# Compression's first product on four column groups of the tensor engine, its partial sums turned and added by one product with a constant

## The reference, cut to what matters

```
nc = (256 - 32) // 16 + 1                       # 15 windows of 32 tokens, 16 apart
def compress(t, pe, w1, w2):                    # t: 256 tokens x 64
    blocks = (t[:, win_idx] + pe).reshape(b, nc, 32 * 64)          # 15 x 2048
    return gelu(blocks @ w1, approximate=False) @ w2               # w1: 2048 x 256, w2: 256 x 64
kc = compress(k_cmp, pe_k, w1_k, w2_k)
vc = compress(v_cmp, pe_v, w1_v, w2_v)
```

## Time and profile before

| | us |
|---|---|
| median of three runs | 2038.98 (2037.13 to 2039.16) |
| the profiled execution | 2038.0 |
| its span | 2036.1 |
| PE busy | 1990.1 (98% of the span) |
| PEld busy | 1821.0 (89%) |
| POOL busy | 1282.7 (63%) |
| DVE busy | 1244.7 (61%) |
| ACT busy | 992.0 (49%) |
| line 659 on PE, 128 matmuls | 29.0 |
| transfers, mean | 166 GB/s |

### The profile page before, as it was taken

How to read it: one execution, slowest core, us unless ns; L and a number is a source line. 1 busy time by engine, 2 the same in 40 slices (tenths; PEclk the granted TensorE clock), 3 DMA queues, 4 the chain that set the end, 5 groups by cost and what they waited for, 6 DMA issues and landing times.

```text
span 2036.1 us, 41550 instructions
## 1 busy us (share of the span) xinstructions
PE 1990.1 (98%) x14222; PEld 1821.0 (89%) x14222; DVE 1244.7 (61%) x2722; ACT 992.0 (49%) x1557; POOL 1282.7 (63%) x622
## 2 busy tenths in 40 slices
PE   9999999999999999999999999999999999999998
PEld 9798998999999888888897889999999998888886
DVE  4463399449999544444454624993599994444444
ACT  5545444654443545544555444446444444455444
POOL 6346689876766555555463466998766665555553
PEclk9999999999999999999999999999999999999999
DMA  6524554554444555556545245545444445555554
GB/s 213 164 92 135 177 175 162 179 169 145 146 141 143 185 195 194 189 194 195 186 142 164 82 148 185 172 160 184 165 146 143 145 142 190 194 193 192 192 196 134
DMA packets 93242, 338.45 MB, mean 166 GB/s; under 512 B 10352, under 2 KB 10736, under 8 KB 93168
## 3 DMA queue, kind: packets, MB, share of 16 engines
q1 hardware_dynamic: 93168, 337.53, 49.8%
HBM read 336.44 MB, written 1.05 MB: 166 GB/s over the span
## 4 chain that ended last, share of the span: by engine, by line
PE 91%; POOL 3%; issue 2%; DVE 2%; ACT 1%; DMA 1%; POOLq 0%; SPq 0%; DVEq 0%; ACTq 0%
PE PS L915 34%; PE PS L852 11%; PE PS L857 11%; PE PS L853 11%; PE PS L551 5%; PE PS L866 4%; POOL WL L454 3%; PE PS L535 2%; PE PS L540 2%; PE PS L536 2%; PE PS L777 2%; PE PS L659 1%; PE PS L517 1%; PE PS L588 1%; PE PS L620 0%
## 5 line engine op out<-in xcount | busy, mean ns | idle before, releaser
L454 POOL TENSOR_TENSOR WL<-ring,WH 128x1024 fp32r<-128x1024 f32 x360 | 908.9, 2531 | 413.6 <-ACT WH L1149 207.9
L1149 ACT CAST WH<-ring 128x1024 fp32r<-128x1024 f32 x512 | 538.0, 1051 | 706.1 <-PE PS L915 327.0
L484 POOL TENSOR_TENSOR HL<-G,HH 128x256 fp32r<-128x256 f32 x256 | 372.6, 1456 | 324.1 <-ACT HH L1251 324.0
L1766 DVE TENSOR_TENSOR WL<-ring,WH 128x1024 fp32r<-128x1024 f32 x248 | 303.8, 1225 | 370.9 <-ACT WH L1149 370.9
L852 PE MATMUL PS<-HH,WH 128*128 128x256 f32 x2048 | 512.2, 288 | 0.0
L853 PE MATMUL PS<-HL,WH 128*128 128x256 f32 x2048 | 501.3, 283 | 0.0
L853 PEld LDWEIGHTS PS<-HL,WH 128*128 128x128 f32 x2048 | 392.2, 192 | 0.0
L852 PEld LDWEIGHTS PS<-HH,WH 128*128 128x128 f32 x2048 | 391.2, 191 | 0.0
L915 PE MATMUL PS<-WH,HH 128*128 128x512 f32 x1024 | 315.5, 389 | 3.0 <-issue 3.0
L915 PE MATMUL PS<-WH,HL 128*128 128x512 f32 x1024 | 315.3, 389 | 0.0
L1715 DVE SCALAR_TENSOR_TENSOR OH<-IOB,slotT,PS 128x384 bf16<-128x384 bf16 x512 | 308.0, 602 | 0.0
(11 more groups left out here) (244 smaller groups left out, 2195.0 us busy)
## 6 DMA issues: line engine op xcount, KB each, us to landing
ring<-stream SPq DMA_DIRECT2D x636, 512.0 KB, 3.3
X<-x_t SPq DMA_DIRECT2D x4, 256.0 KB, 3.5
out_t<-X SPq DMA_DIRECT2D x2, 512.0 KB, 2.7
CN<-consts SPq DMA_DIRECT2D x1, 843.5 KB, 9.4
WF<-last SPq DMA_DIRECT2D x1, 512.0 KB, 9.8
PR<-params SPq DMA_DIRECT2D x2, 239.0 KB, 5.0
CN<-consts SPq DMA_DIRECT2D x1, 64.0 KB, 4.3
```

The source lines that it names most:

```text
L454: nc.gpsimd.tensor_tensor(WL[:, b, :], ring[:, slot, :], WH[:, b, :].bitcast(F32), ALU.subtract).then_inc(done, 1)
L484: nc.gpsimd.tensor_tensor(GL[:, s, :], G[:, tile, :], GH[:, s, :].bitcast(F32), ALU.subtract).then_inc(L.gl_ready, 1)
L1149: nc.scalar.copy(WH[:, b, :], ring[:, slot, :]).then_inc(L.hi_ready, 1)
L1766: V.tensor_tensor(WL[:, s % 2, :], ring[:, (U0 + s) % SLOTS, :], WH[:, s % 2, :].bitcast(F32), ALU.subtract).then_inc(L.vlo_ready, 1)
```

## The change

The four chunks of a piece now go to four groups of 32 columns of the array (`tile_position`), and so to partitions 0 to 14, 32 to 46, 64 to 78 and 96 to 110 of bank 7. Each group adds up its own chunk of the four pieces. Each product now writes 32 partitions, since `BL` is widened from 15 to 32 columns, of which 17 are zero, set by POOL at the layer's start (one more memset, and one more wait on PE for it). The four partial sums have to be added before the gelu. So ACT first copies all 128 partitions of bank 7 to `HID`; behind projection 11 PE multiplies `HID` by a constant 128 x 15 with ones where partition mod 32 equals the window (`sum4`), which turns and adds in one; the gelu moves to the two instructions that fill `HV`.

```diff
@@ shape_constants
+    put("sum4", p % 32 == np.arange(NCMP)[None, :])
@@ POOL, start of a layer
+                    nc.gpsimd.memset(BL[:, :, :, NCMP:32], 0.0).then_inc(padded, 1)
                     nc.gpsimd.memset(HV[:, :, :, :, :], 0.0).then_inc(padded, 1)
@@ PE
                         pe.wait_ge(L.blocks_ready, i + 1)
-                        o = bank[7][0:NCMP, i * 256:(i + 1) * 256]
+                        pe.wait_ge(padded, 2 * layer + 1)
                         for k in range(4):
                             w = piece(2 * W1 + 4 * i + k).rearrange("p (j m) -> p j m", j=CHUNKS // 4)
                             for j in range(CHUNKS // 4):
-                                mm = nc.tensor.matmul(o, BL[:, i, CHUNKS // 4 * k + j, :], w[:, j, :],
-                                                      start=(k == 0 and j == 0), stop=(k == 3 and j == CHUNKS // 4 - 1))
+                                mm = nc.tensor.matmul(bank[7][32 * j:32 * j + 32, i * 256:(i + 1) * 256],
+                                                      BL[:, i, CHUNKS // 4 * k + j, :], w[:, j, :],
+                                                      start=(k == 0), stop=(k == 3), tile_position=(0, 32 * j))
...
                     for i in range(4):
-                        mm = nc.tensor.transpose(bank[7][:, 16 * i:16 * i + NCMP],
-                                                 HID[0:NCMP, i // 2, i % 2 * P:(i % 2 + 1) * P], ident[0:NCMP, 0:NCMP])
+                        mm = nc.tensor.matmul(bank[7][:, 16 * i:16 * i + NCMP],
+                                              HID[:, i // 2, i % 2 * P:(i % 2 + 1) * P], cn("sum4"), start=True, stop=True)
@@ ACT
                     act.wait_ge(L.piece_done, 2 * W1 + 8)
-                    nc.scalar.activation(HID[0:NCMP, :, :], bank[7][0:NCMP, :].rearrange("p (s n) -> p s n", s=2),
-                                         ACT.Gelu).then_inc(L.hid_ready, 1)
+                    nc.scalar.copy(HID[:, :, :], bank[7].rearrange("p (s n) -> p s n", s=2)).then_inc(L.hid_ready, 1)
                     take(11)
...
-                    nc.scalar.copy(HV[:, 0, :, 0, 0:NCMP], hid[:, 0]).then_inc(L.hid_ready, 1)
-                    nc.scalar.copy(HV[:, 1, :, :, 0:NCMP], bc(hid[:, 1], 2, NH)).then_inc(L.hid_ready, 1)
+                    nc.scalar.activation(HV[:, 0, :, 0, 0:NCMP], hid[:, 0], ACT.Gelu).then_inc(L.hid_ready, 1)
+                    nc.scalar.activation(HV[:, 1, :, :, 0:NCMP], bc(hid[:, 1], 2, NH), ACT.Gelu).then_inc(L.hid_ready, 1)
```

More of the change, by code:

```diff
@@ L89 @@
                       ("cr", 128), ("sr", 128), ("c16", 32), ("s16", 32), ("cmpneg", 64), ("any", 2),
-                      ("blkd", 4), ("iota", 129)):
+                      ("blkd", 4), ("sum4", 15), ("iota", 129)):
     CONSTS[_name] = (_at, _at + _width)
@@ L332, in program @@
         K2 = region(2 * SEQ).rearrange("p (s n) -> p s n", s=2)
-        BL = region(2 * CHUNKS * NCMP).rearrange("p (s j c) -> p s j c", s=2, j=CHUNKS)
+        BL = region(2 * CHUNKS * 32).rearrange("p (s j c) -> p s j c", s=2, j=CHUNKS)
         HV = region(2 * 2 * P).rearrange("p (s b h c) -> p s b h c", s=2, b=2, h=NH)
@@ L1078, in _ @@
                     act.wait_ge(L.piece_done, 2 * W1 + 8)
-                    nc.scalar.activation(HID[0:NCMP, :, :], bank[7][0:NCMP, :].rearrange("p (s n) -> p s n", s=2),
-                                         ACT.Gelu).then_inc(L.hid_ready, 1)
+                    nc.scalar.copy(HID[:, :, :], bank[7].rearrange("p (s n) -> p s n", s=2)).then_inc(L.hid_ready, 1)
                     take(11)
-                    act.wait_ge(padded, layer + 1)
+                    act.wait_ge(padded, 2 * layer + 2)
                     act.wait_ge(hid_tr, layer + 1)
                     hid = bank[7][:, 0:64].rearrange("p (s b c) -> p s b c", s=2, b=2)[:, :, :, 0:NCMP]
-                    nc.scalar.copy(HV[:, 0, :, 0, 0:NCMP], hid[:, 0]).then_inc(L.hid_ready, 1)
-                    nc.scalar.copy(HV[:, 1, :, :, 0:NCMP], bc(hid[:, 1], 2, NH)).then_inc(L.hid_ready, 1)
+                    nc.scalar.activation(HV[:, 0, :, 0, 0:NCMP], hid[:, 0], ACT.Gelu).then_inc(L.hid_ready, 1)
+                    nc.scalar.activation(HV[:, 1, :, :, 0:NCMP], bc(hid[:, 1], 2, NH), ACT.Gelu).then_inc(L.hid_ready, 1)
                     probabilities(PT[0])
@@ L1462, in _ @@
                             src = k2[:, 0, :, hi:hi + NCMP]
-                            ins = V.tensor_tensor(BL[:, s, 8 * hi:8 * hi + 8, :], src,
+                            ins = V.tensor_tensor(BL[:, s, 8 * hi:8 * hi + 8, 0:NCMP], src,
                                                   bc(pr(pe_name, 8 * hi, 8 * hi + 8), 2, NCMP), ALU.add)
```

## The result

The changed kernel takes 2041.68 us in the median of 20 runs (2037.91 to 2045.06), the kernel before, measured beside it, 2037.93 (2036.90 to 2040.28, 20 runs). The ratio is 1.0019, 95% interval [1.0013, 1.0026]: slower by 3.9 us by the ratio, where 3.6 us less were forecast. The time lies inside the range, within 0.1 us of the rivals "the clock" and "no overlap" (2041.6 both), but it moved the wrong way. The profiled execution has a span of 2041.2 us, 5.1 above that of before.

What follows compares the result with a forecast made beforehand. PE is busy 98%, but the path runs through bursts, DVE's masks and ACT to projection 11, then mostly ACT. Gain 3.11 less 1.30 gives 1.8 us a layer, 3.6 in all: 2038.0 becomes 2034.4; range 2033.4 to 2042.0.

Steps and rivals of the forecast that it cites:

- the clock: Rival, 13%: PE's new idle gaps around burst 2 and projection 11 drop it to 1.2 GHz, costing 3.1 us a layer; 2041.6.
- no overlap: Rival, 9%: the array takes one column group at a time, nothing is saved, the table load adds 1.3 a layer; 2041.6.
- Column groups overlap, a burst saves 2.5 us: Compression bursts on PE: four column groups work at once, so each burst of 16 matmuls saves 2.5 us.
- Burst 1 saves nothing, DVE's copy decides: Behind burst 1: it ends at 59.6 instead of 62.2, but the scores still wait for DVE until 62.47; saved, nothing.
- The second chain moves by 2.5 us: From burst 2's scores through DVE's masks and ACT's exponentials to projection 11's first `WH`: all comes 2.5 us earlier.
- Projection 11 starts 3.55 us earlier, POOL takes back 0.44: Projection 11 on PE starts at 73.40 instead of 76.95, then waits 0.44 us for POOL's `WL`; gain 3.11 us.
- ACT's load costs 1.30 and hides the product: Behind projection 11: gelu's table load and gelu instructions cost ACT 1.30 us; the load hides PE's product with the constant.
- Transfers cost nothing: Pieces for projection 11 land by 72.7, before ACT wants them at 73.4; no cost, though above 6.6 us would count.

Runs made afterwards that it cites:

- spins: Changed kernel plus, in each layer, 10 spare float32 products on PE behind burst 1 and 9 ahead of projection 11; 2037.87 us, ratio 0.9997.
- one_group: Changed kernel without its column groups, all chunks in the first 32 columns, the new work behind projection 11 kept; 2043.00 us, ratio 1.0020.
- spin_first: Changed kernel plus 10 spare products behind burst 1 only, none ahead of projection 11; ratio 1.0004.
- table_early: Changed kernel plus one tiny gelu on ACT behind the copy into HID, to load the table during projection 11; 2038.85 us, ratio 1.0002.
- groups_tail: Changed kernel with the constant's product between projection 11's pieces, an early table load and both gelu moved, no spare products; 2040.50 us, ratio 1.0006.
- early_tail: ahead_tail with HID copied by DVE between block scores, the constant's product and both gelu moved earlier, 11 spare products; 2030.75 us, ratio 0.9962.
- spins_table: Changed kernel with spare products in both gaps and the early tiny gelu that loads the table; 2035.83 us, ratio 0.9988.
- ahead_tail: groups_tail with bursts 1 and 2 ahead of all window scores, and 5 and 12 spare products; 2031.83 us, ratio 0.9968.

## Why the prediction was wrong

*Column groups overlap, a burst saves 2.5 us.* Right: 3.63 us became 1.07, a saving of 2.56 at full clock.

*Burst 1 saves nothing, DVE's copy decides.* Right in place, and the cause of the trouble: the 2.64 us that it saves PE are idle.

*The second chain moves by 2.5 us.* This is the step that failed. It took each duration behind burst 1 from a profile at full clock. At half clock scores, burst 2 and scores took the 2.5 us back: 12.32 and 11.58 in place of 10.05 for the first exponential, 10.01 in the kernels of this order where the gap was filled. The idle time in which it fell stood in the forecast, but its cost was put at nothing in the sum.

*Projection 11 starts 3.55 us earlier, POOL takes back 0.44.* Right at full clock (3.49 at its start, 3.13 at the first `WL` product in spins). In the changed kernel the clock fell a second time here; its first `WL` product comes at 20.64 from burst 1, 0.4 behind that of before.

*ACT's load costs 1.30 and hides the product.* Too low. In one_group the tail costs 1.79, in spin_first's full-clock layer 1.57 (24.89 - 21.26 against 26.36 - 24.30). The load starts only when the product is there.

*Transfers cost nothing.* Nearly: the two pieces of projection 11, asked for while others were in flight, took 5.6 and 6.4 us to land, the longest in that stretch of before having been 5.9. `WH` waited for them 0.1 and 0.26 us, the second of which is as in the kernel before (0.24). In layer 1 burst 4 waited 1.48, idle time of PE that the forecast did not have.

*The rivals.* The clock had 13% and was the case. Its price, 3.1 us a layer, was near: 28.33 - 24.89 = 3.44 in layer 0, 3.35 in layer 1. The first fall alone held the first exponential back by 2.3 and 1.6 us, where 1.6 had been priced. That its time, 2041.6, was met to 0.1 us is luck. It stood for a loss of 2 x (3.1 - 1.8) = 2.6 us, counted from the 2038.98 of three runs, and the kernel before then measured 1.05 less. The loss itself was 3.9; with the prices as measured it comes out at 2 x (3.4 - 1.5) = 3.8. What should have raised its chance stood in my own sum: 5 of 10.4 us saved on PE were called waiting, in a stretch where no wait of that length had been. And the kernel before has spare products on PE (line 508) in other stretches.

What stays open: why the clock fell behind a gap of 1.5 us in one execution and not behind 2.65 us in another (table_early, layer 1). The Trainium skill ("TensorE: Matmul & The Clock Gate", Part 1) explains a run-to-run spread by a monitor that runs free of the kernel. That would fit the 7.2 us over which the changed kernel's 20 runs spread; no run here tests it.

## What to carry to other kernels

Before a product is made faster, ask what PE will do in the time won: if the path goes on through another engine, the time becomes idle, and behind an idle gap of 2 to 3 us the clock can be half for the work that follows, which here cost more (3.4 us a layer) than the products saved (3.1). Fill such gaps, first with work that is needed later (here the next burst and the product with the constant), and only what is left with spare products. These are work too: where the clock had fallen all the same, nine of them held PE for 3.7 us and the next projection with it. And ask what the instruction that a table load serves waits for: the load started only behind that wait here. One small call of the function earlier, where ACT has time, takes it off the path.

## What the runs showed of the hardware

- Four column groups of float32 products run side by side: 16 matmuls in 0.69 us from first start to last in the changed kernel, 3.25 before. Four start within 0.02 us, which is out of program order if a product's two halves are issued together.
- A clock fall showed behind idle gaps of 1.45, 1.5 and 1.55 us too, not always, and never in the profile of before, whose longest gap is 1.67 us; it held behind 1.44 us in layer 1 of one_group and behind 2.65 in that of table_early. The runs of the three kernels that have column groups, the changed order and no gap filled (changed, table_early, groups_tail) spread over 7.2, 8.3 and 10.8 us, those of before over 3.4 in its 20 beside the changed kernel, those of early_tail over 0.6.
- A table load waits for the semaphores of the instruction that it serves (0.23 us of idle time in the changed kernel, 0.41 in one_group, ended by the product). Where the table was loaded early, in spins_table, the gelu itself waited, 0.24 us.
- A 512 KB piece that was asked for with two others in flight took 5.6 and 6.4 us to land in the changed kernel, with three others 6.6 there and 7.2 in ahead_tail, against a median of 3.3 in the stretch of before.
